# The FFN's input becomes the split of g times x1, and the second norm's factor moves behind the up projection

## What is computed

```python
def rms_norm(x, g):
    y = xf * lax.rsqrt(jnp.mean(xf * xf, axis=-1, keepdims=True) + EPS)
    return y * g
...
    x = x + rms_norm(mixed, g_mix_post)                       # "x1" in this text
    f, conv_state = conv_ffn(rms_norm(x, g_ffn_pre), conv_prefix, w_up, conv_w, conv_b, w_down)
    x = x + rms_norm(f, g_ffn_post)
...
def conv_ffn(h, prefix, w_up, conv_w, conv_b, w_down):
    up = h @ w_up                                             # 1024 -> 2 * 2816
    ext = jnp.concatenate([prefix, up], axis=1)
    c = conv_b + sum(ext[:, j:j + T] * conv_w[j] for j in range(CONV_WIDTH))   # 3 taps
    gate, val = jnp.split(c, 2, axis=-1)
    return (jax.nn.gelu(gate) * val) @ w_down, ext[:, -(CONV_WIDTH - 1):]
```

## Time and profile before

| | us |
|---|---|
| median of the runs | 1868.93 |
| the profiled execution | 1867.63 |
| its span on the core | 1865.9 |
| TensorE busy in the span | 1817.3 |
| VectorE busy | 826.0 |
| ScalarE busy | 559.3 |
| GpSimd busy | 276.7 |

### The profile page before, as it was taken

How to read it: one execution, slowest core, us unless ns; L and a number is a source line. 1 busy time by engine, 2 the same in 40 slices (tenths; PEclk the granted TensorE clock), 3 DMA queues, 4 the chain that set the end, 5 groups by cost and what they waited for, 6 DMA issues and landing times.

```text
span 1865.9 us, 28821 instructions
## 1 busy us (share of the span) xinstructions
PE 1817.3 (97%) x11113; PEld 1722.3 (92%) x11113; DVE 826.0 (44%) x1079; ACT 559.3 (30%) x882; POOL 276.7 (15%) x321
## 2 busy tenths in 40 slices
PE   6999999999999999999999999999999999999998
PEld 6878787879699899999999879999999999999997
DVE  5565657575334423232242584442134442344436
ACT  5565757471100100000032452221022220122224
POOL 1121212120133211111110220000000010100002
PEclk9999999999999999999999999999999999999999
DMA  5202020205411111111131031111111111111312
GB/s 166 69 24 68 23 68 23 68 23 175 119 44 47 34 51 51 57 34 41 49 137 57 12 137 45 46 54 47 45 45 45 44 40 52 45 45 51 134 31 97
DMA packets 162283, 113.74 MB, mean 61 GB/s; under 512 B 5389, under 2 KB 152213, under 8 KB 161947
## 3 DMA queue, kind: packets, MB, share of 16 engines
q1 hardware_dynamic: 161035, 108.34, 19.5%
q10 hardware_dynamic: 1200, 4.75, 0.7%
HBM read 95.86 MB, written 13.40 MB: 59 GB/s over the span
## 4 chain that ended last, share of the span: by engine, by line
PE 87%; ACT 5%; DVE 4%; issue 2%; DMA 1%; SPq 0%; ACTq 0%; POOL 0%; DVEq 0%; POOLq 0%
PE ps L1484 67%; PE ps L1494 10%; PE misc L1576 3%; PE misc L1470 1%; ACT zl L736 1%; ACT zl L741 1%; PE ps L1750 1%; PE ps L1560 1%; ACT att L753 1%; PE ps L1561 1%; PE ps L1564 1%; PE ps L1566 1%; DVE hn L1334 1%; PE ps L1470 0%; DMA kv_pg<-in_cache_v 0%
## 5 line engine op out<-in xcount | busy, mean ns | idle before, releaser
L1074 DVE TENSOR_TENSOR w_lo<-stage,w_hi 128x1024 fp32r<-128x1024 f32 x148 | 198.4, 1341 | 579.6 <-POOL w_hi L561 579.2
L1484 PE MATMUL ps<-h_hi,w_lo 128*128 128x344 f32 x1896 | 404.2, 322 | 0.8 <-DVE y_lo L1272 0.8
L1484 PE MATMUL ps<-h_lo,w_hi 128*128 128x344 f32 x1896 | 402.8, 321 | 0.0
L1484 PE MATMUL ps<-h_hi,w_hi 128*128 128x344 f32 x1896 | 400.7, 320 | 0.0
L561 POOL TENSOR_SCALAR w_hi<-stage 128x1024 fp32r<-128x1024 f32 x148 | 158.4, 1070 | 1263.1 <-PE ps L1484 1059.6
L1484 PEld LDWEIGHTS ps<-h_hi,w_lo 128*128 128x128 f32 x1896 | 319.5, 188 | 2.9 <-issue 1.4
L1484 PEld LDWEIGHTS ps<-h_lo,w_hi 128*128 128x128 f32 x1896 | 321.2, 189 | 0.0
L1484 PEld LDWEIGHTS ps<-h_hi,w_hi 128*128 128x128 f32 x1896 | 316.3, 188 | 0.0
L967 ACT ACTIVATE up<-ps 128x1032 f32<-128x1032 f32 x44 | 45.5, 1034 | 354.6 <-PE ps L1484 352.9
L1494 PE MATMUL ps<-h_hi,w_lo 128*128 128x344 f32 x408 | 136.7, 335 | 0.0
L1494 PE MATMUL ps<-h_lo,w_hi 128*128 128x344 f32 x408 | 131.0, 321 | 0.0
(11 more groups left out here) (269 smaller groups left out, 2521.1 us busy)
## 6 DMA issues: line engine op xcount, KB each, us to landing
stage<-in_w_in SPq DMA_DIRECT2D x48, 512.0 KB, 3.8
stage<-in_w_up SPq DMA_DIRECT2D x44, 512.0 KB, 3.8
stage<-in_w_down SPq DMA_DIRECT2D x16, 448.0 KB, 3.4
stage<-in_w_branch SPq DMA_DIRECT2D x24, 256.0 KB, 2.7
x_scratch<-trunk SPq DMA_DIRECT2D x1, 4128.0 KB, 12.6
x_back<-x_scratch SPq DMA_DIRECT2D x1, 4128.0 KB, 13.0
x_tok<-in_x_prompt SPq DMA_DIRECT2D x8, 512.0 KB, 8.3
kv_pg<-in_cache_k SPq DMA_DIRECT2D x16, 256.0 KB, 3.6
```

The costliest lines, as they stand in the source:

```text
L1074: V.tensor_tensor(w_lo[par][:, :, :], stage[par][:, :, :], w_hi[par][:, :, :].bitcast(F32), ALU.subtract).then_inc(w_lo_made, 1)
L1484: last = M(ps[par][:, c, :], w[par][:, k, :], x[:, c * CH:(c + 1) * CH], start=(k == 0 and s == 0), stop=(k == n - 1 and s == 2))
```

## The change

Five things change, all in the stretch above but for the last:

1. The FFN's input is the split of g * x1, without the second factor: ScalarE writes `h_hi` = round(g * x1) straight from `trunk` (`x1_use`), and VectorE makes `h_lo` = x1 * g - `h_hi` in one scalar_tensor_tensor. `hn` and its 24 instructions on VectorE are gone.
2. The order on VectorE is `ffn_input(c)` per chunk, in which the multiply, the add of x and the `h_lo` of two tiles earlier alternate. Chunk 0's `h_lo` no longer waits for the second factor. Both `split_lo` of the first two units stand behind `ffn_input(0)`.
3. GpSimd adds the squares in pairs (`pair_squares`), 12 instructions of 344 columns, between its adds of x. TensorE sums 4 tiles per chunk in place of 8, into a bank of `misc`, and in other places: behind all of chunk 0's products, behind chunk 1's, and inside chunk 2's. The first two up units' chunk 0 runs one unit after the other.
4. ScalarE's order is new: it makes `h_hi` and the square of a tile together, and chunk 1 follows `rstd_m(2)`.
5. In the up stages VectorE evicts the unit, multiplied by the whole `rstd`, into `up`. ScalarE then makes `tails` and `conv` from `up` in SBUF.

```diff
@@ gpsimd @@
+            def pair_squares(n):
+                a, b = (x_sq[(2 * n + i) % len(x_sq)] for i in range(2))
+                pool.wait_ge(xsq_made, 2 * n + 2)
+                nc.gpsimd.tensor_tensor(a, a, b, ALU.add).then_inc(sq_paired, 1)
+
             for c in range(NCH):
                 for k in range(0, KT, 2):
                     pool.wait_ge(mr_made, c * KT + k + 1)
...
                     nc.gpsimd.tensor_tensor(trunk[:, k, cols[c]], trunk[:, k, cols[c]], x_t[:, k, cols[c]], ALU.add
                                             ).then_inc(x1_even, 1)
+                    if k > 0 or c > 1:
+                        pair_squares(c * (KT // 2) + k // 2 - 1)
                 if c == 0:
                     for j in range(2):
                         split_hi(j, 16 * (U_UP[0] // 2 + 1), U_UP[0] + j)
+                        if j == 0:
+                            pair_squares(KT // 2 - 1)
+            pair_squares(NCH * KT // 2 - 1)
@@ scalar @@
+            def x1_use(c, first, end):
+
                 for k in range(first, end):
                     j = c * KT + k
                     act.wait_ge(x1_odd if k % 2 else x1_even, c * (KT // 2) + k // 2 + 1)
+                    A(h_hi[:, k, cols[c]], trunk[:, k, cols[c]], ACT.Copy, scale=g_ffn[:, k:k + 1]).then_inc(hn_hi, 1)
                     if j >= len(x_sq):
-                        act.wait_ge(sx_used, j + 1 - len(x_sq))
+                        act.wait_ge(sx_used, (j - len(x_sq)) // 2 + 1)
...
+            x1_use(0, 5, 7)
+            rstd_m(1)
+            x1_use(0, 7, KT)
+            m_part_out(5)
+            rstd_m(2)
+            x1_use(1, 0, 5)
             rstd_x(0)
...
-                        act.wait_ge(unit_done, j * 2 + (U_UP[g] + k + 1))
-                        A(chunks(up[k][:, :]), ps[k], ACT.Copy)
-                        A(tails[:, f, :].rearrange("p o t -> p (o t)"), last_cols(k, TAIL), ACT.Copy)
-                        A(chunks(conv[k][:, :]), ps[k], ACT.Identity, bias=conv_par[:, 3, f],
-                          scale=conv_par[:, 2, f]).then_inc(ps_free[k], 1)
+                        act.wait_ge(ps_free[k], j + freed(f"up{g}", k, 1))
+                        A(tails[:, f, :].rearrange("p o t -> p (o t)"), up[k][:, T - TAIL:T], ACT.Copy)
+                        A(conv[k][:, :], up[k][:, :], ACT.Identity, bias=conv_par[:, 3, f],
+                          scale=conv_par[:, 2, f]).then_inc(up_scaled, 1)
@@ vector @@
+            def ffn_input(c):
                 dve.wait_ge(rm_made, c + 1)
+                for k in range(KT + 2):
                     if k < KT:
+                        V.tensor_tensor(trunk[:, k, cols[c]], trunk[:, k, cols[c]], rstd[:, cols[c]], ALU.mult
+                                        ).then_inc(mr_made, 1)
...
+                        if k % 2:
+                            dve.wait_ge(mr_made, c * KT + k + 1)
+                            V.tensor_tensor(trunk[:, k, cols[c]], trunk[:, k, cols[c]], x_t[:, k, cols[c]], ALU.add
+                                            ).then_inc(x1_odd, 1)
+                    if k > 1:
+                        dve.wait_ge(hn_hi, c * KT + k - 1)
+                        V.scalar_tensor_tensor(h_lo[:, k - 2, cols[c]], trunk[:, k - 2, cols[c]], g_ffn[:, k - 2:k - 1],
+                                               h_hi[:, k - 2, cols[c]].bitcast(F32), ALU.mult, ALU.subtract
+                                               ).then_inc(h2_made, 1)
+                    if c == 0 and k == 5:
+                        add_part_squares(1)
 
             add_part_squares(0)
-            residual(0)
-            add_part_squares(1)
+            ffn_input(0)
             split_lo(0, U_UP[0])
-            ffn_h(0)
             add_part_squares(2)
-            residual(1)
-            residual(2)
-            ffn_h(1)
-            ffn_h(2)
+            split_lo(1, U_UP[0] + 1)
+            ffn_input(1)
+            ffn_input(2)
...
+                        dve.wait_ge(unit_done, j * 2 + (U_UP[g] + k + 1))
+                        dve.wait_ge(rx_made, NCH)
+                        V.tensor_tensor(chunks(x[:, :]), ps[k], chunks(rstd), ALU.mult).then_inc(ps_free[k], 1)
                         split_lo(k, j * 2 + (U_UP[g] + k + 2))
-                        dve.wait_ge(ps_free[k], j + freed(f"up{g}", k, 1))
+                        dve.wait_ge(up_scaled, j * 2 + (2 * f0 + k + 1))
@@ tensor @@
+            for par in range(2):
+                pe.wait_ge(w_lo_made, U_UP[0] + par + 3)
+                for k in range(KT):
+                    up_products(0, k, par)
+                if par == 0:
                     mean_squares(2)
+            x1_square_sums(0)
+            for k in range(KT):
+                for par in range(2):
+                    up_products(1, k, par)
+            x1_square_sums(1)
+            for k in range(5):
+                for par in range(2):
+                    up_products(2, k, par)
+            pe.wait_ge(rx_made, 1)
+            for k in range(5, KT):
+                up_products(2, k, 0)
+            x1_square_sums(2)
+            for k in range(5, KT):
+                up_products(2, k, 1)
```

More of the change, by code:

```diff
@@ L248, in build @@
         x_t = sb("x_t", [P, KT, T], F32, s_res)
-        hn = [sb(f"hn{i}", [P, CH], F32, s_res) for i in range(3)]
-        x_sq = [sb(f"x_sq{i}", [P, CH], F32, s_res)[:, :] for i in range(3)]
+        x_sq = [sb(f"x_sq{i}", [P, CH], F32, s_res)[:, :] for i in range(5)]
         x_sq += [work[2][:, i * CH:(i + 1) * CH] for i in range(NCH)]
@@ L300, in build @@
         late = slice(Y_WHOLE * P, T)
+        sx_bank = [misc[:, i * 512:i * 512 + CH] for i in range(2)]
         x1_dram = nc.dram_tensor("x1_scratch", [P, KT, T], F32, kind="Internal").ap()
@@ L335, in build @@
             pool_edge, pool_pre, pool_d, ya_ps, y_hi_made, mix_made, yb_made, mhi_made, m_split,
-            sq_made, ss_added, xr_in, mr_made, hn_made, hn_hi, h2_made, x1_out, conv_step,
+            sq_made, ss_added, xr_in, mr_made, sq_paired, hn_hi, h2_made, up_scaled, x1_out, conv_step,
             gelu_made, gv_made, g_hi_made, g_made, tail_ps, tail_sb, x1r_in, yr_made, yt_ps,
@@ L353, in build @@
             "mix_made", "yb_made", "mhi_made", "m_split", "sq_made", "ss_added", "xr_in", "mr_made",
-            "hn_made", "hn_hi", "h2_made", "x1_out", "conv_step", "gelu_made", "gv_made",
+            "sq_paired", "hn_hi", "h2_made", "up_scaled", "x1_out", "conv_step", "gelu_made", "gv_made",
             "g_hi_made", "g_made", "tail_ps", "tail_sb", "x1r_in", "yr_made", "yt_ps", "yt_left",
@@ L899, in rstd_of @@
                 A(rstd[:, cols[c]], rstd[:, cols[c]], ACT.Exp, scale=-0.5).then_inc(made, 1)
-            LN_ORDER = [("m", 0), ("x1", 0), ("m", 1), ("m", 2), ("x1", 1), ("x1", 2)]
+            LN_ORDER = [("m", 0), ("m", 1), ("m", 2), ("x1", 0), ("x1", 1), ("x1", 2)]
             def rstd_m(c):
@@ L907, in rstd_x @@
             def rstd_x(c):
-                act.wait_ge(sx_used, (c + 1) * KT)
-                rstd_of(c, rx_made, LN_ORDER.index(("x1", c)) + 1, ps[1][:, c, :])
-            def x1_squares(c, first, end):
+                act.wait_ge(sx_used, (c + 1) * KT // 2)
+                rstd_of(c, rx_made, LN_ORDER.index(("x1", c)) + 1, sx_bank[c % 2])
+            def x1_use(c, first, end):
                 for k in range(first, end):
@@ L919, in x1_squares @@
                     A(x_sq[j % len(x_sq)], trunk[:, k, cols[c]], ACT.Square).then_inc(xsq_made, 1)
[L921 to L924, removed]
             with act.Fori(0, KT // 2 - 2) as i:
@@ L940, in _ @@
             rstd_m(0)
-            x1_squares(0, 0, KT // 2)
+            x1_use(0, 0, 2)
             m_part_out(3)
-            x1_squares(0, KT // 2, KT)
-            rstd_x(0)
[L945 to L952, removed]
+            x1_use(0, 2, 5)
+            m_part_out(4)
+            x1_use(0, 5, 7)
[4 more added lines that the diff above has]
+            x1_use(1, 0, 5)
+            rstd_x(0)
+            x1_use(1, 5, KT)
+            x1_use(2, 0, 5)
             rstd_x(1)
-            x1_squares(2, len(x_sq) - 1, KT)
-            h_out(1)
+            x1_use(2, 5, KT)
             rstd_x(2)
-            h_out(2)
             for g, (f0, size) in enumerate(FFN_GROUPS):
@@ L1309, in add_part_squares @@
                                     ).then_inc(ss_added, 1)
-            def residual(c):
+            def ffn_input(c):
                 dve.wait_ge(rm_made, c + 1)
[L1314 to L1330, removed]
-                    if k < KT:
[L1332 to L1339, removed]
+                for k in range(KT + 2):
+                    if k < KT:
+                        V.tensor_tensor(trunk[:, k, cols[c]], trunk[:, k, cols[c]], rstd[:, cols[c]], ALU.mult
+                                        ).then_inc(mr_made, 1)
+                        if c == 0 and k == 1:
+                            dve.wait_ge(xg_sb, len(XT_GROUPS))
+                        if k % 2:
```

(25 more changed lines are left out.)

## The result

| kernel | median, us | runs | against the kernel before |
|---|---|---|---|
| before | 1868.55 | 4 | |
| changed | 1883.03 (1880.47 to 1884.56) | 4 | 1.0076, interval 1.0064 to 1.0089 |

The change costs 14.5 us; 11.8 us were forecast, 1880.7 from a median of 1868.93, to which a fourth run of the kernel before has come since.

A forecast was written before the change was run, and what follows sets the result against it. TensorE was taken as the bound, busy 1817.3 of 1865.9 us. Unit 2's start +9.8, the clock +1.5 and up-stage ends +0.5 sum to +11.8; on the median 1868.93 that gives 1880.7 us, range 1871 to 1886.5.

The forecast's parts named there:

- The chain through SyncE's queue: Ahead of unit 2: its weights queue behind the copy of x1, landing 15.5 us after x's last add; start +9.8 us.
- the copy doesn't hold the weights: Rival at unit 2: weights land in time however late x1 is; 1869.4 us; within the 0.10 for no change.
- GpSimd and VectorE exclude each other: Before x's last add: instructions reading two SBUF tiles run one after the other, 0.74 us per GpSimd add or pair.
- the bound of 1875.8: Lower bound if GpSimd does not hold off a scalar_tensor_tensor: last add of x 4.9 us earlier, +6.9.
- The waits at the head of chunk 1: VectorE waits there for `h_hi`, 3.1 us, then 2.3 us more through ScalarE's square needing a buffer.
- 1.5 more for the clock: Unit 0's chunk 0, ahead of `mean_squares(2)`: TensorE's low clock after a 4.5 us wait costs 1.5 us.
- The clock behind the idle: At unit 2's start: TensorE's clock is low after an idle of 12 us, +1.5 us.
- The ends of the up stages: VectorE's eviction, then `tails` and `conv` on ScalarE, delay the first tap by 0.25 us, twice: +0.5.
- 21 `h_lo` at 0.49: VectorE's work ahead of the last add of x: these instructions were put at 10.1 us.
- about 1873: Lower bound if a scalar_tensor_tensor is not held off and chunk 1's waits are gone: little more than 4 us left.
- The 1.56 us that the low clock costs before: In the kernel before, 12 products after TensorE's 4.61 us wait for `w_lo` run at low clock, costing 1.56 us.

The follow-up runs named there:

- e1: The changed kernel with the weights of up units 2 and 3 issued ahead of the copy of x1 to DRAM; 1871.84 us.
- e4: The kernel before with one more wait on SyncE, holding the copy of x1 until `h_lo` of chunk 2's tile 4 is made; 1881.73 us.
- e2: The changed kernel without GpSimd's 12 additions of squares in pairs, TensorE summing all 24 squares; 1874.87 us.
- e3: The changed kernel with the sums of chunk 0's squares moved ahead of unit 1's products of chunk 0; 1880.53 us.
- e5: The kernel before with the weights of up units 2 and 3 issued ahead of the copy of x1; 1868.72 us.
- e7: The changed kernel with the edits of e1 and e3, and unit 0's `w_hi` and `w_lo` made before chunk 0's last two tiles; 1866.34 us.
- e8: The kernel of e7 without GpSimd's pairs, TensorE summing all 24 squares; 1864.67 us.
- e6: The kernel of e1 with ScalarE evicting the second and third FFN groups as before, the second norm's factor left out there; 1869.16 us.

## Why the prediction held, step by step

- **The chain through SyncE's queue.** Right, and decisive: the last add of x to the landing was put at 15.5 us and is 15.6; unit 2 starts 18.2 us behind the last add, forecast 17.9. e1 takes the chain off the path and 11.2 us go; e4 puts it onto the path of the kernel before and 12.7 us come. The rival "the copy doesn't hold the weights" fell with both.
- **GpSimd and VectorE exclude each other.** Right. e2 prices 11 pairs at 7.5 us where 8.1 was in the sum. A scalar_tensor_tensor took 1.35 us for 0.56 beside a GpSimd instruction, so the bound of 1875.8 that rested on the contrary had no ground. The Trainium skill (SBUF — State Buffer, Who interferes with whom) says that a VectorE instruction with two SBUF inputs contends with a GpSimd one that reads SBUF. The trace agrees for this instruction too.
- **The waits at the head of chunk 1.** The mechanism is right, the size was 1.1 us short: 4.28 and 2.21 us measured, 3.1 and 2.3 forecast. The term that was mis-sized is "1.5 more for the clock" ahead of `mean_squares(2)`. The low clock behind TensorE's wait there lasted 5.9 us (from 1064.95 to 1070.8), over 20 products that take 3.1 at full clock: 2.7 us. That covers the difference between 53.5 and 54.5 for the last add of x. It need not come out so each time: in e3, whose program is the changed kernel's up to there, the low clock lasted 4.3 us and cost 2.0, and VectorE's first wait was 3.62. In e1 they were 4.4, 2.1 and 3.65, and the last add of x came at 53.9.
- **A wait that I had not named**, TensorE's 2.4 us for `add_part_squares(1)`, which now stands between two multiplies. It cost nothing here. Behind it the clock was low for 3.4 us in the changed kernel and full for over 5 us in e1; TensorE's next wait was 3.8 us in the one and 5.4 in the other, and chunk 0 began 18.75 and 18.8 us from the first multiply, since VectorE sets the pace there.
- **The clock behind the idle, 1.5 us.** Measured 1.5, and that is luck: behind idles of 8.3 us (e2), 11.9 us (e3) and 10.2 us (e4) at the same place the clock was low for 5.1, 4.8 and 5.6 us, which costs 2.3, 2.2 and 2.5.
- **The ends of the up stages, +0.5.** Measured +1.1 (2.4 against 1.3). The eviction starts at 1769.99, the first tap at 1772.92: 2.93 us where before it was 2.39. I had started `conv` 0.06 us behind `tails` and let it take up to 1.26; it starts 0.17 behind and takes 1.25, and each hand-over between the engines adds 0.14.

```profile
1769.99 1.23 DVE L1357 TENSOR_TENSOR up<-ps,work 128x1032 f32<-128x1032 f32 x1 [5.59 <-PE ps L1481]
1771.24 1.23 DVE L1080 TENSOR_TENSOR w_lo<-stage,w_hi 128x1024 fp32r<-128x1024 f32 x1
1772.92 1.28 DVE L1361 SCALAR_TENSOR_TENSOR conv<-up,par_t,conv 128x1023 f32<-128x1023 f32 x1 [0.45 <-ACT conv L975]
```

```profile
1771.36 0.21 ACT L974 ACTIVATE tails<-up 128x10 f32 x1 [9.95 <-DVE up L1357]
1771.53 1.25 ACT L975 ACTIVATE conv<-up,par_t 128x1032 f32<-128x1032 f32 x1
```

- **Slips in the working.** 21 `h_lo` at 0.49 are 10.3 us, not 10.1. The lower bound "about 1873" does not follow from its terms: 6.9 less the waits' 4.7 leaves 2.2 us, 1871. The 1.56 us that the low clock costs before lie off the path: in e5 it lasts 6.2 us there, and unit 2 starts at 61.7 all the same.
- **Not accounted for**: 0.5 us of the profiled difference, and about 0.8 of the medians' 14.5.

The change takes out 11.8 us of VectorE's instructions in this stretch (`hn`) and 7 us of TensorE's sums. With the order put right (e7, e8) it does pay, up to 4.3 us, and most without the pairs.

## What to carry to other kernels

When a tile is made later, follow every DMA that waits for it, and then what stands behind that DMA in the same queue: here a store that nothing on TensorE waits for in this stretch delayed the weights that TensorE needed next. e1 cured it by order within the queue; whether another queue would have done as well no run tries. Work moved to GpSimd is not free for VectorE when both read two tiles from SBUF; price the time that each holds VectorE off, 0.7 us here for a pair of 344 columns. And savings on TensorE count only where TensorE is not already waiting: here three edits of order and dropping one of the two savings made a loss of 14.5 us a gain of 4.3.

## What was unexpected of the hardware

How long TensorE stays at its lower clock behind a wait varied even with the same wait ahead of it. The same wait of 4.61 us, at the same place of the kernel before with two orders of its DMAs, ends in e4 and e5 with these rows; the last of each pair is the first product that starts at full rate, 0.16 us ahead of the next:

```profile
1063.68 0.65 PE L1813 MATMUL ps<-h_hi,w_lo 128*128 128x344 f32 x1 [4.61 <-DVE w_lo L1075]
...
1066.68 0.32 PE L1813 MATMUL ps<-h_lo,w_hi 128*128 128x344 f32 x1
```

```profile
1064.98 0.65 PE L1813 MATMUL ps<-h_hi,w_lo 128*128 128x344 f32 x1 [4.61 <-DVE w_lo L1075]
...
1071.17 0.32 PE L1813 MATMUL ps<-h_hi,w_lo 128*128 128x344 f32 x1
```

That is 3.0 us over 10 products in the one and 6.2 us over 21 in the other, a cost of 1.4 and 2.9 us; before, it was 1.6. The order of the DMAs alone doesn't explain it: e1, with the same order as e5, was low for less time at this place than the changed kernel, 4.4 for 5.9 us. Behind a wait of 2.4 us ahead of unit 2 the clock fell in e8 (0.71 over 3.4 us) but not in e7, e6 or e1. What sets the length stays open. So one profile doesn't give the price of such a step: here it lay anywhere between nothing and 2.9 us, and a forecast can hold it only to within some 1.5 us.
